# Where two groups of turned inputs, a table load and two small sums stand in a two-block transformer kernel

## The reference

```python
def first_block(x, meta_tokens, w_in, ...):
    h = jnp.concatenate([meta, x], axis=1)
    ...
        u = rms_norm(h, mix_pre_g[l])
        proj = u @ w_in[l]
        ...
        gate_a, gate_b = jnp.split(jax.nn.sigmoid(gates + b_gate[l]), 2, axis=-1)
        mixed = (gate_a * y_a + gate_b * y_b) @ w_out[l]
        h = h + rms_norm(mixed, mix_post_g[l])
        u = rms_norm(h, ffn_pre_g[l])
        gt, up = jnp.split(u @ w_ffn_in[l], 2, axis=-1)
        h = h + rms_norm((jax.nn.silu(gt) * up) @ w_ffn_out[l], ffn_post_g[l])
    return h[:, N_META:, :]

def conformer_conv_branch(a, g, z, w_dw, b_dw, ln_g, ln_b):
    u = a * jax.nn.sigmoid(g)
    u = lax.conv_general_dilated(u, ...) + b_dw
    u = jax.nn.silu(layer_norm(u, ln_g, ln_b))
    return u * jax.nn.silu(z)

def second_block(x, ...):
    ...
        proj = jnp.einsum('bld,de->ble', h, w_in[l])
        y_conv = conformer_conv_branch(a, g, zc, ...)
        y_attn = dsa_sparse_attention(q, k, v, qi, ki, wi, topk) * jax.nn.silu(za)
        y = jnp.einsum('ble,ed->bld', jnp.concatenate([y_conv, y_attn], axis=-1), w_out[l])
        h = layer_norm(DEEPNORM_ALPHA * h + y, post_ln_g[l], post_ln_b[l])
```

## Time and profile before

| | |
|---|---|
| median of 3 runs | 889.29 us (887.88 to 890.0) |
| the profiled execution | 888.76 us |
| its span in the profile | 886.6 us |
| busy: PE, PEld, DVE, ACT, POOL | 98%, 94%, 57%, 54%, 70% |
| mean granted clock of TensorE | 0.995 of full |

### The profile page before, as it was taken

One profiled execution on the slowest core, in us unless ns is written; L12 is line 12 of the kernel. 1 busy time (PEld: TensorE's weight loads), 2 busy tenths in 40 slices (PEclk: granted clock), 3 DMA queues, 4 the chain that ended last, 5 costly groups with the idle time before them and its releaser, 6 DMA issues.

```text
span 886.6 us, 17110 instructions
## 1 busy us (share of the span) xinstructions
PE 868.9 (98%) x6815; PEld 835.6 (94%) x6815; DVE 501.3 (57%) x1117; ACT 479.4 (54%) x941; POOL 624.2 (70%) x361
## 2 busy tenths in 40 slices
PE   9999999999999998999999999999999999999996
PEld 7988999999999998999999999999988999999886
DVE  4413111699827847544331014878975668789674
ACT  5547655632356557544444455445568564456773
POOL 5823755555556987999998889866784877766353
PEclk9999999999999999999999999999999999999998
DMA  9625534333432565465555673744410627644201
GB/s 280 203 79 183 178 99 140 116 123 97 142 98 94 179 221 171 143 191 190 191 161 165 191 208 101 239 144 143 144 64 33 184 56 210 184 134 155 96 1 48
DMA packets 134622, 128.09 MB, mean 144 GB/s; under 512 B 6512, under 2 KB 132336, under 8 KB 134544
## 3 DMA queue, kind: packets, MB, share of 16 engines
q1 hardware_dynamic: 134064, 126.20, 45.7%
q10 hardware_dynamic: 480, 0.79, 0.3%
HBM read 125.80 MB, written 1.05 MB: 143 GB/s over the span
## 4 chain that ended last, share of the span: by engine, by line
PE 87%; POOL 4%; DVE 3%; ACT 3%; issue 2%; POOLq 0%; DVEq 0%; ACTq 0%
PE PS L627 22%; PE PS L629 22%; PE PS L628 22%; PE PS L908 3%; PE PS L618 2%; PE PS L675 1%; PE PS L671 1%; PE PS L672 1%; PE PS L1054 1%; PE PS L811 1%; POOL w_lo L1225 1%; PE PS L870 1%; PE PS L733 1%; POOL u_t L1253 1%; POOL x_lo L1235 1%
## 5 line engine op out<-in xcount | busy, mean ns | idle before, releaser
L1225 POOL TENSOR_TENSOR w_lo<-ring,w_hi 128x1024 fp32r<-128x1024 f32 (+2 forms) x237 | 544.3, 2311 | 192.5 <-ACT w_hi L1387 182.6
L627 PE MATMUL PS<-x_hi,w_hi 128*128 128x256 f32 (+2 forms) x1442 | 423.3, 294 | 0.9 <-ACT zoneA L1370 0.6
L629 PE MATMUL PS<-x_hi,w_lo 128*128 128x256 f32 (+2 forms) x1442 | 409.7, 284 | 0.0
L628 PE MATMUL PS<-x_lo,w_hi 128*128 128x256 f32 (+2 forms) x1442 | 408.9, 284 | 0.0
L1387 ACT ACTIVATE w_hi<-ring 128x1024 fp32r<-128x1024 f32 (+1 forms) x235 | 237.6, 1015 | 72.1 <-PE PS L629 68.8
L627 PEld LDWEIGHTS PS<-x_hi,w_hi 128*128 128x128 f32 (+1 forms) x1442 | 271.5, 188 | 3.5 <-issue 0.7
L628 PEld LDWEIGHTS PS<-x_lo,w_hi 128*128 128x128 f32 (+1 forms) x1442 | 270.8, 188 | 1.4 <-issue 0.2
L629 PEld LDWEIGHTS PS<-x_hi,w_lo 128*128 128x128 f32 (+1 forms) x1442 | 271.2, 188 | 0.0
L2213 DVE SCALAR_TENSOR_TENSOR PS<-zoneA,cols,PS 128x256 f32<-128x256 f32 x240 | 98.7, 482 | 0.1
L1370 ACT ACTIVATE zoneA<-PS 128x272 f32<-128x272 f32 (+3 forms) x76 | 29.2, 384 | 104.7 <-PE PS L629 104.7
L1370 ACT ACTIVATE zoneB<-PS 128x256 f32<-128x256 f32 (+4 forms) x115 | 40.9, 378 | 68.2 <-DVE PS L2180 37.9
(11 more groups left out here) (339 smaller groups left out, 1332.9 us busy)
## 6 DMA issues: line engine op xcount, KB each, us to landing
ring<-in_w_in SPq DMA_DIRECT2D x58, 1024.0 KB, 5.4
ring<-in_w_ffn_in SPq DMA_DIRECT2D x22, 1024.0 KB, 5.1
ring<-in_w_out SPq DMA_DIRECT2D x12, 1024.0 KB, 5.0
ring<-in_w_ffn_out SPq DMA_DIRECT2D x16, 704.0 KB, 4.5
ring<-in_w_mla_o SPq DMA_DIRECT2D x4, 1024.0 KB, 5.2
ring<-in_w_hg_o SPq DMA_DIRECT2D x4, 1024.0 KB, 5.0
ring<-in_w_kv_b SPq DMA_DIRECT2D x2, 1024.0 KB, 5.4
ring<-in_w_q_b SPq DMA_DIRECT2D x2, 768.0 KB, 4.9
```

The source lines that it names most:

```text
L627: mm(out_, hi_w, hi_x, start=start, stop=False)
L628: mm(out_, hi_w, lo_x, start=False, stop=False)
L629: return mm(out_, lo_w, hi_x, start=False, stop=stop)
L1225: sub(lo_w, src, hi_w, ALU.subtract).then_inc(sem("w_lo"), 1)
```

## The change

Three edits.

*Input groups.* Group 0 is turned between the chunks mix 6 and mix 7, group 1 between the two halves of the token sums, group 2 behind them, then comes the turned inverse, then group 3. They use banks 0 and 1 in turn (before 0, 1, 3, 0). ACT copies group 0 behind the rounding that follows mix 6, group 1 behind the square of mix 7, and groups 2 and 3 behind the root. The rounding that stood behind the root now stands behind `x_hi` of c = 1.

*Sigmoid.* `warm(ACT.Sigmoid)` is added ahead of each layer of the second block.

*Convolution's sums.* In the attention's loop the part of the gate chunk now comes ahead of the two sums, in both layers.

```diff
-ORDER += [part(n, c) for n in ("hgo", "mix") for c in range(DC)]
-ORDER += [("x", i) for i in range(4)]
+ORDER += [part("hgo", c) for c in range(DC)]
+ORDER += [part("mix", c) for c in range(DC - 1)] + [("x", 0), part("mix", DC - 1)] + [("x", i) for i in range(1, 4)]
...
-    BANK[CHUNK["x", _i]] = (0, 1, 3, 0)[_i]
+    BANK[CHUNK["x", _i]] = _i % 2
...
-            def linear_norm(tag, chunks):
+            def linear_norm(tag, chunks, between=None):
...
+                if between:
+                    between()
                 pe.wait_ge(sem(f"sq_{tag}"), DC)
...
+            def turn_x(i):
+
+                if i == 0:
+                    pe.wait_ge(sem("late_in"), 64)
+                g = CHUNK["x", i]
+                bank_free(g)
+                for c in (2 * i, 2 * i + 1):
+                    for t in range(2):
+                        at = (2 * (c % 2) + t) * P
+                        last = nc.tensor.transpose(PS[:, BANK[g], at:at + P], x_again[:, t, c * P:(c + 1) * P], ident)
+                done(last)
...
-                           for c in range(2, DC)])
...
+                           for c in range(2, DC - 1)]
+                        + [lambda: turn_x(0), lambda: chunk(*part("mix", DC - 1), X, META, free=(sem("sq_post"), DC - 4))],
+                        between=lambda: turn_x(1))
+            turn_x(2)
+            inverse_turned(1)
+            turn_x(3)
...
+                    if l == 0 and s < 2:
+                        turns_over(2 - s, BANK[CHUNK[part(f"{T}za", 2)]])
+                    for n, m, first, end in z_chunks(l, s):
+                        chunk(*part(f"{T}{n}", m), X, q_from, first=first, end=end)
                     if s == CLN_STEP[l] + 2:
                         pe.wait_ge(sem("cln_added"), 4 * l + 2)
...
-                if c == DC - 1:
-                    token_std("post")
-                round_piece(ENDS[g] + PAIRS)
...
+                if c < DC - 1:
+                    round_piece(ENDS[g] + PAIRS)
+                if c in (DC - 2, DC - 1):
+                    take_x(c - DC + 2)
+            token_std("post")
+            take_x(2)
+            take_x(3)
...
-                if c < 2:
-                    take_x(2 + c)
-                else:
+                if c == 1:
+                    round_piece(ENDS[CHUNK[part("mix", DC - 1)]] + PAIRS)
+                if c >= 2:
                     square_mid(c - 2)
...
+            warm(ACT.Sigmoid)
```

More of the change, by code:

```diff
@@ L1132, in _ @@
                             .then_inc(sem(f"sum_{T}cln"), 1)
[L1133 to L1136, removed]
                 pe.wait_ge(sem("att_o_out"), 2 * l + 2)
@@ L1614, in _, with take_x @@
                       (sem("y_first"), HEADS + c + 1))
+            def take_x(i):
+                take("x", i, hT[:, 2 * i:2 * i + 2, META:L], n=2 * SEQ, view=lambda s: s.rearrange("p (c t) -> p c t", c=2))
             for c in range(DC):
@@ L1619, in _ @@
                         lambda: act.wait_ge(sem("chunk_done"), g + 1), SEQ, added=True)
-                if c == DC - 1:
-                    token_std("post")
-                round_piece(ENDS[g] + PAIRS)
-            def take_x(i):
-                take("x", i, hT[:, 2 * i:2 * i + 2, META:L], n=2 * SEQ, view=lambda s: s.rearrange("p (c t) -> p c t", c=2))
+                if c < DC - 1:
[5 more added lines that the diff above has]
+            take_x(3)
             def square_mid(c):
                 af(f_sq[:, c, :], hT[:, c, META:L], ACT.Square).then_inc(sem("sq_fpre"), 1)
-            take_x(0)
-            take_x(1)
             for c in range(DC):
```

## The result

The changed kernel takes 891.17 us in the median of 20 runs (890.08 to 893.27), the kernel before 889.25 us in 20 runs beside them (887.87 to 892.75). The ratio is 1.0024, with a 95% interval of 1.0017 to 1.003: slower by 0.17% to 0.3%, at the edge of what can be told from no change. The forecast was 890.8 us, in a range of 889.0 to 893.6. The profiled execution took 891.34 us, with a span of 889.5: 1.84 us lie around the span, where it was 2.16. On the page TensorE's busy time is up by 1.0 us.

What follows compares the result with a forecast made beforehand. TensorE, busy 98% of the span, was taken as the bound. Input groups +2.12, Sigmoid 0 and convolution's sums -0.56 gave +1.56 us on the median of 889.29: 890.8 us, range 889.0 to 893.6.

Steps and rivals of the forecast that it cites:

- The chain behind the root: Input groups' stretch: root 0.66 us later, then each step on ACT, DVE and POOL timed to w_lo's end at 349.80.
- The lower bound's case: Input groups: root only 0.45 us later, next steps as before; loss 1.8 us.
- The wait: First feed-forward chunks: PE waits some 3.5 us for POOL's x_lo; low products of c = 1 start at 350.58, +2.12 us.
- The supply: Behind that wait: `low(2)` held to 350.25, x_lo of c = 7 at 355.2, slack 0.35 us, so nothing added.
- Part 2: Early Sigmoid table, second block's layer starts: load already ahead of the copy's wait; sum 0, ends 0 and +0.1 us.
- Part 3: Convolution's sums behind the gate chunk: -0.56 us in layer 0's attention (ends 0 and -0.9), 0 in layer 1.
- the clock falls in the new wait: Rival, feed-forward chunks: PE's 3.5 us idle halves the clock, 3.0 us more (bound 4.6), 893.8 us; chance 14%.
- The forecast's sign for the forecast case: Trace sign at PE's new wait in the feed-forward chunks: granted clock 1.00 around 350 us.
- POOL in the way: Its rival, POOL not in the way: x_lo of c = 1 at its old distance, gain 0.5, 888.2 us; chance 9%.

Runs made afterwards that it cites:

- fewer_dummies: Changed kernel with 13 unread matmuls of 128 columns in TensorE's wait ahead of the low products of c = 1; 890.09 us, ratio 1.0012 to before.
- round_behind_root: Changed kernel with the last weight piece's rounding moved back directly behind the root; 887.82 us, ratio 0.9988 to before.
- table_alone: Kernel before with only the two early Sigmoid instructions added; one execution, 890.32 us.
- pool_takes_x_lo_first: Changed kernel with GpSimd computing x_lo of c = 1 before its last w_lo piece; 889.2 us, ratio 1.0008 to before.

## Why the prediction came out as it did

*The chain behind the root: right, step by step.* The forecast had the root at 342.54, `product(0)` at 343.60, `added(1)` at 345.06, u_t at 345.51, x_hi of c = 1 at 345.92, the rounding from 346.32, POOL's w_lo from 347.44 to 349.80. Measured: 342.50, 343.55, 345.02, 345.46, 345.88, 346.28, 347.40 to 349.75. Group 0 cost PE 0.4 us (L710 at 340.97, before 340.60), forecast 0.45. The lower bound's case, a root that comes only 0.45 later, did not happen.

*The wait.* Low products of c = 1: forecast 350.58 with +2.12, measured 350.67 with +2.21 by the first traces, and +2.32 for the whole stretch without falls on either side (fewer_dummies against the first trace of before). The term of +2.12 was 0.1 to 0.2 too small.

*The supply: right.* `low(2)` was held until 350.03 (forecast 350.25). The Trainium skill (SBUF — State Buffer, Who interferes with whom) says that a DVE instruction with two SBUF inputs contends with a GpSimd instruction that reads SBUF, and that the one waits for the whole of the other. This trace agrees, with 2.28 us where a free one takes 0.48. POOL's x_lo of c = 7 came at 354.23 (forecast 354.4), and in fewer_dummies, with the clock up, no bracket stands behind the low products.

*Part 2: right within the span*, at 0, with the copy not delayed. The forecast took the 2.16 us around the span as fixed; they became 1.8, a gain of 0.3 that it had no term for. *Part 3: the size right, the split not.* Forecast -0.56, measured -0.55 (-0.54 to -0.58 in the pairs). The first sum did start when the old one had (660.41 by its shift), but the next attention step gained 0.38 and not 0.56 (664.80 less the shift of 3.82 is 660.98, before 661.36), the one behind the second sum 0.36 more, and 0.20 were given back where TensorE waits for DVE, now 0.42 and before 0.30. In layer 1 the second sum no longer waits, and nothing came of it, as forecast; but not through a longer wait at 844.91, as the text had it: that is 0.29 (0.28 before). The gain is gone at 846.26 already, where the step starts 0.62 behind the row ahead of it, before 0.33.

*The rival "the clock falls in the new wait": its mechanism was true and was given 14%.* The forecast's sign for the forecast case was 1.00 around 350; it was 1.00 there and 0.51 from 351.8. What failed is the argument against it, "PE's 2.33 us of rest did not trigger it here", together with the row of 1.00 in the old wait. Both were read from one execution. The row was true, but where the fall comes it begins near the rest's end or behind it, and of five traces of that stretch four have it. The price was wrong too: 1.53 us, not 3.0, since a fall of 3.4 us at half the clock can cost no more than half of its length. The Trainium skill (TensorE: Matmul & The Clock Gate, HAM oscillation — how this bites in real kernels) warns of idle gaps of PE, behind which the work starts at the low clock. The trace agrees, with 0.51 behind a rest of 3.27 us.

That the time still fell on the forecast is in part luck, of two kinds. The first lies on the other side of the comparison: the kernel before pays the same in most traced executions, 1.33 to 1.52 us (38.59 to 38.78 against 37.26). Between executions with a fall the stretch grew from 38.6 to 38.8 (before) to 41.11 (after), so by 2.3 to 2.5, which less 0.55 for part 3 gives 1.8 to 2.0. The median span grew by some 2.2: it is 889.3 after, and before the median time of 889.25 less the usual 2.12 is 887.1, an estimate. The second is outside the span, where part 2's 0.3 came off: 2.2 less 0.3 is the medians' 1.92. Between the first traces alone the spans differ by 3.84 - 0.55 - 0.4 for the end that differs by execution, so by 2.9. Against the forecast's +1.56 the span's 2.2 is 0.6 too much. Of it 0.1 to 0.2 is the wait's term; the rest would be the executions in which before had no fall while after had one. That last is an inference from nine traces and the runs' clocks, not measured by itself.

*POOL in the way: yes.* The rival at 9% is refuted by the order turned on POOL, which moved the wait, and by round_behind_root, which shows what that rival would have given: 887.8 (it said 888.2).

## What to carry to other kernels

When an instruction is moved on one engine, ask who on another engine has its consumer queued ahead of something urgent: here one rounding of 1.05 us on ACT, moved behind the second x_hi, put a piece of 2.35 us of GpSimd in front of the operand that TensorE needed next. A wait that is taken out uncovers the next one, so follow every other engine's queue to the end of the stretch. And read a clock, or any state of the chip, from several executions before an argument rests on its absence.

## What the runs showed of the hardware

- A fall of the granted clock at a rest of TensorE is decided per execution: at 2.33 us in 4 of 5 traces of one and the same stretch, at 3.25 to 3.27 us in 2 of 2, at 2.03 and 2.08 us in 2 of 2 (both behind an earlier fall), at 1.24 to 1.34 us in 3 of 8. It began between 0.4 us before and 1.4 us after TensorE took up its work, and lasted 3.4 us at 0.51. It cost 1.3 to 1.5 us where TensorE was the bound, 0.14 where a wait for GpSimd took the place of the fall (37.40 against 37.26), and nothing ahead of a wait. The cause of its coming or not in one execution stays open, and so does the part that the one-column matmuls and transposes ahead of the 1.24 and 2.33 us rests have in it.
- With small matmuls in the rest the clock stayed up in three traces out of three, and once without them (pool_takes_x_lo_first, with rests of 1.24, 1.37 and 0.81 us). One of 128 columns on these float32 operands shows as two instructions of 0.11 us.
- A fall of 6.8 us near 11 us into the program goes with a first stretch longer by 2.4 to 2.9 us. It was traced in the kernel before (twice); table_alone has one of 3.4 us there, with 1.0 us. No edit here touches it.
- A table load on ACT took 1.28 us and the next ACTIVATE began 0.01 to 0.02 us behind it; no further pause was seen.
- The time less the span was 2.06 to 2.26 us in 68 executions without the early Sigmoid, and 1.75 to 1.91 us in 70 of 72 with it.
